# Parts of 576, 768 and 768 tokens in the feed-forward stage, in place of three of 704

## The reference

```
z = rms_norm(x, g) @ w_in;  u, q, k, v = column groups of z
h = x + concat(pool_mixer(u), banded_attention(q, k, v)) @ w_out
hn = rms_norm(h, norm_ffn)
y = h + (silu(hn @ w_gate) * (hn @ w_up)) @ w_down
```

## Time and profile before

| | us |
|---|---|
| median of 3 runs | 2101.21 |
| profiled execution | 2103.07 |
| its span, first to last instruction | 2101.3 |
| TensorE matmul busy | 2075.9 (99%) |
| VectorE busy | 1277.1 (61%) |
| ScalarE busy | 884.0 (42%) |
| GpSimd busy | 777.9 (37%) |

### The profile page before, as it was taken

How to read it: one execution, slowest core, us unless ns; L and a number is a source line. 1 busy time by engine, 2 the same in 40 slices (tenths; PEclk the granted TensorE clock), 3 DMA queues, 4 the chain that set the end, 5 groups by cost and what they waited for, 6 DMA issues and landing times.

```text
span 2101.3 us, 33467 instructions
## 1 busy us (share of the span) xinstructions
PE 2075.9 (99%) x12470; PEld 1885.5 (90%) x12470; DVE 1277.1 (61%) x2070; ACT 884.0 (42%) x2149; POOL 777.9 (37%) x503
## 2 busy tenths in 40 slices
PE   8999999999999999999999999999999999999999
PEld 7888888877888899999998999999998999999997
DVE  5655555553222566766666766766667767666665
ACT  6766666653334533333333433333334333333331
POOL 0000000034324544354435653445445643544352
PEclk9999999999999999999999999999999999999999
DMA  7011111033774532333224523333224422222222
GB/s 189 29 41 41 39 39 41 24 101 112 219 243 148 171 108 89 110 106 109 78 77 151 189 88 108 108 106 90 95 81 159 161 81 70 72 81 72 70 80 75
DMA packets 243401, 212.89 MB, mean 101 GB/s; under 512 B 21149, under 2 KB 220618, under 8 KB 243242
## 3 DMA queue, kind: packets, MB, share of 16 engines
q1 hardware_dynamic: 243242, 210.76, 32.6%
HBM read 170.03 MB, written 40.79 MB: 100 GB/s over the span
## 4 chain that ended last, share of the span: by engine, by line
PE 93%; ACT 2%; DVE 1%; issue 1%; SPq 1%; DMA 1%; POOL 0%; DVEq 0%; ACTq 0%; POOLq 0%
PE ps L813 27%; PE ps L815 27%; PE ps L814 27%; PE ps L914 2%; PE ps L888 2%; PE ps L1030 1%; PE ps L900 1%; PE ps L832 1%; SPq L466 1%; PE ps L1032 1%; PE ps L1028 1%; PE ps L876 1%; ACT s_sb L1208 1%; PE ps L931 1%; PE ps L940 0%
## 5 line engine op out<-in xcount | busy, mean ns | idle before, releaser
L746 POOL TENSOR_TENSOR w_lo<-w_lo_raw,w_hi 128x512 fp32r<-128x512 f32 (+1 forms) x240 | 393.3, 1645 | 606.5 <-PE ps L815 412.7
L813 PE MATMUL ps<-xs_hi,w_hi 128*128 128x352 f32 x1848 | 596.5, 323 | 3.6 <-POOL w_lo L746 2.8
L815 PE MATMUL ps<-xs_lo,w_hi 128*128 128x352 f32 x1848 | 597.8, 324 | 0.0
L813 PEld LDWEIGHTS ps<-xs_hi,w_hi 128*128 128x128 f32 x1848 | 347.6, 188 | 5.7 <-POOL w_lo L746 3.1
L815 PEld LDWEIGHTS ps<-xs_lo,w_hi 128*128 128x128 f32 x1848 | 351.0, 190 | 0.0
L1718 DVE TENSOR_TENSOR h<-ps,h 128x512 f32<-128x512 f32 (+1 forms) x396 | 270.3, 688 | 118.4 <-PE ps L815 112.1
L814 PE MATMUL ps<-xs_hi,ws_lo 128*128 128x352 f32 x1056 | 339.6, 322 | 0.0
L746 POOL TENSOR_TENSOR ws_lo<-ws_lo_raw,w_hi 128x512 fp32r<-128x512 f32 x204 | 295.3, 1449 | 112.2 <-DVE ws_lo_raw L1561 68.4
L1275 ACT ACTIVATE w_hi<-ws_lo_raw 128x512 fp32r<-128x512 f32 x264 | 165.5, 628 | 326.2 <-DVE ws_lo_raw L1561 326.0
L813 PE MATMUL ps<-w_hi,act_hi 128*128 128x512 f32 x660 | 257.2, 390 | 2.6 <-DVE act_lo L1641 2.6
L814 PE MATMUL ps<-w_hi,act_lo 128*128 128x512 f32 x660 | 256.9, 389 | 0.0
(11 more groups left out here) (142 smaller groups left out, 3248.0 us busy)
## 6 DMA issues: line engine op xcount, KB each, us to landing
w_lo_raw<-in_w_gate SPq DMA_DIRECT2D x66, 512.0 KB, 5.1
w_lo_raw<-in_w_up SPq DMA_DIRECT2D x66, 512.0 KB, 5.2
w_lo_raw<-in_w_down SPq DMA_DIRECT2D x66, 512.0 KB, 4.1
xload<-in_x_prompt SPq DMA_DIRECT2D x16, 512.0 KB, 4.2
mix_d<-o_st SPq DMA_DIRECT2D x64, 128.0 KB, 1.8
xt_lo_raw<-mix_d SPq DMA_DIRECT2D x16, 512.0 KB, 6.0
wg_hi_raw<-in_x_prompt SPq DMA_DIRECT2D x16, 512.0 KB, 5.1
h_d<-wg_hi_raw SPq DMA_DIRECT2D x16, 512.0 KB, 2.6
```

The costliest lines, as they stand in the source:

```text
L746: nc.gpsimd.tensor_tensor(lo, raw, hi.bitcast(F32), ALU.subtract).then_inc(done, 1)
L813: nc.tensor.matmul(out, s_hi, m_hi, start=first, stop=False, skip_group_check=partial)
L815: return nc.tensor.matmul(out, s_hi, m_lo, start=False, stop=final, skip_group_check=partial)
```

## The change

The parts now have 576, 768 and 768 tokens (`T_OF`), and products 288, 384 and 384 columns (`NB_OF`). 576 is 4 x 128 + 64, and 768 is 6 x 128: only part 0 has a tile of 64 rows. The last tile of the last part holds 64 prompt tokens and the 64 sample tokens and is stored by two transfers. Tiles in SBUF are sized for the largest part; the high and low token blocks share one array of 14 slots, and the low block of product 6 of part 0 lies in unused columns of the high slots 3 to 6. For that the high blocks 3 to 6 of part 1 wait for the last product of part 0 (`rows_high`). The weight buffers lie elsewhere, so `load_down(0)` is issued behind the last `store_hn` and the wait for `h_stored`, and three waits on the output projection's last products (`wo_free`) are moved by a step. At the joint behind part 0, `accumulate` makes low block 4 before the additions of the tile of 64 rows.

```diff
@@ -53,13 +53,17 @@
-PARTS = 3
-T = TOKENS // PARTS
-NB = T // 2
+T_OF = (576, 768, 768)
+FIRST = (0, 576, 1344)
+PARTS = len(T_OF)
+NB_OF = tuple(n // 2 for n in T_OF)
+T, NB = max(T_OF), max(NB_OF)
+HALF_TILE = T_OF[0] // PART
-PT_TILES = 6
-D_UNITS = 2 * PT_TILES
+TILES_OF = tuple(-(-n // PART) for n in T_OF)
+PT_TILES = max(TILES_OF)
@@ -253,13 +257,12 @@
+                sb("between", [PART, 1312], scope=project)
-            xs_hi = sb("xs_hi", [PART, PRODUCTS, HALF_K, NB], F32R, scope=ffn)
-            xs_raw, xs_lo = twin("xs_lo", [PART, PRODUCTS, HALF_K, NB], ffn)
-            sb("rest", [PART, PART], scope=ffn)
+            xs_raw, xs_split = twin("xs", [PART, 2 * PRODUCTS, HALF_K * NB], ffn)
@@ -268,15 +271,15 @@
-            act_hi = sb("act_hi", [PART, 2, T + DEC], F32R, scope=ffn)
+            act_hi = sb("act_hi", [PART, 2, T], F32R, scope=ffn)
+            odd = twin("w2_lo1", [PART, 2, 2, HALF_K * PART], ffn)
+            sb("gap", [PART, PART], scope=ffn)
+            even = twin("w2_lo0", [PART, 2, 2, HALF_K * PART], ffn)
-            odd = twin("w2_lo1", [PART, 2, 2, HALF_K * PART], ffn)
-            sb("gap", [PART, 960], scope=ffn)
-            even = twin("w2_lo0", [PART, 2, 2, HALF_K * PART], ffn)
@@ -407,11 +410,18 @@
-            return (DEC if j == PT_TILES - 1 else PART), T * p + PART * j
+            return min(PART, T_OF[p] - PART * j), FIRST[p] + PART * j
-            return y_sample[0] if a == SEQ else y_prompt[0, a:a + rows, :]
+            end = min(a + rows, SEQ)
+            both = [(y_prompt[0, a:end, :], 0, end - a)]
+            return both + ([(y_sample[0], end - a, rows)] if a + rows > SEQ else [])
+        def y_stores(p, j):
+            return sum(len(y_rows(b, j)) * (1 + ((b, j) == (PARTS - 1, LAST_TILE))) for b in range(p) if j < TILES_OF[b])
...
@@ -449,14 +462,33 @@
-            return xs_raw[:, m]
+            return lows_of(xs_raw, p, m)
+        def block_in(t, p, slot):
+            return t[:, slot, 0:HALF_K * NB_OF[p]].rearrange("p (k n) -> p k n", k=HALF_K)
+        def xs_hi(p, m):
+            return block_in(xs_split, p, m)
+        def lows_of(t, p, m):
+            if p == 0 and m == PRODUCTS - 1:
+                return t[:, 3:3 + HALF_K, HALF_K * NB_OF[0]:(HALF_K + 1) * NB_OF[0]]
+            return block_in(t, p, PRODUCTS + m)
+        def xs_lo(p, m):
+            return lows_of(xs_split, p, m)
-            return (0, 1, 2, 3, 5, 4) if G == NG - 1 else tuple(range(PT_TILES))
+            return (0, 1, 2, 3, 5, 4) if G == NG - 1 else tuple(range(TILES_OF[G // GROUPS]))
+        def d_units(G):
+            return sum(2 * TILES_OF[g // GROUPS] for g in range(G))
-            return D_UNITS * G + 2 * tiles_of(G).index(j) + nh
+            return d_units(G) + 2 * tiles_of(G).index(j) + nh
...
@@ -662,7 +695,7 @@
-                need(sp, d_ready, D_UNITS * G)
+                need(sp, d_ready, d_units(G))
@@ -711,10 +744,10 @@
                     load_gate_up(0)
                 if i == 7:
                     load_first_rows()
-            load_down(0)
             store_hn(NTILES - 1)
             for b in range(3):
                 sp.wait_ge(h_stored[b], 16 * len(range(b, NTILES, 3)))
+            load_down(0)
             for b in range(2):
                 sp.wait_ge(hn_stored[b], 16 * len(range(b, NTILES, 2)))
             for G in range(NG):
@@ -732,11 +765,11 @@
+                    for i in range(TILES_OF[p]):
...
@@ -961,7 +994,7 @@
-                    if i == NTILES - 1 and nh == 1 and c in (1, 4):
+                    if i == NTILES - 1 and nh == 1 and c in (1, 3, 4):
...
@@ -1011,14 +1044,14 @@
-                    pe.wait_ge(al_done, 4 * G + (3 if PART * (j + 1) <= NB else 4))
+                    pe.wait_ge(al_done, 4 * G + (3 if PART * (j + 1) <= NB_OF[G // GROUPS] else 4))
-                        if j < PT_TILES - 1:
+                        if (G // GROUPS, j) != (0, HALF_TILE):
@@ -1265,7 +1298,7 @@
-                    act.wait_ge(wo_free, 1)
+                    act.wait_ge(wo_free, 1 if m < 4 else 2)
@@ -1275,14 +1308,15 @@
-                    act.wait_ge(product_done, after_product(last_set(p), m))
+                    act.wait_ge(product_done, after_product(last_set(p), PRODUCTS - 1 if p == 1 and m >= 3 else m))
...
@@ -1317,7 +1351,8 @@
-                nc.scalar.activation(act_hi[:, c, NB * l:NB * (l + 1)], aa[:, n % 2, :], ACT.Copy).then_inc(ah_done, 1)
+                nb = NB_OF[G // GROUPS]
+                nc.scalar.activation(act_hi[:, c, nb * l:nb * (l + 1)], aa[:, n % 2, 0:nb], ACT.Copy).then_inc(ah_done, 1)
@@ -1550,7 +1585,7 @@
-                    dve.wait_ge(wo_free, 1 if n == 0 else 2)
+                    dve.wait_ge(wo_free, 2 if n == 0 else 3)
...
@@ -1587,58 +1622,62 @@
-                if l == 1:
-                    nc.vector.tensor_tensor(hi[:, T:T + DEC], aa[:, n % 2, NB - DEC:NB], hi[:, T - DEC:T].bitcast(F32),
+                if l == 1 and G < GROUPS:
+                    nc.vector.tensor_tensor(hi[:, t:t + DEC], aa[:, n % 2, nb - DEC:nb], hi[:, t - DEC:t].bitcast(F32),
...
@@ -1705,9 +1744,11 @@
+                        if j == HALF_TILE and TILES_OF[p] == HALF_TILE + 1:
+                            rows_low(p + 1, j)
-                        dve.wait_ge(h_loaded[j], 16 * (p + 1))
+                        dve.wait_ge(h_loaded[j], 16 * sum(j < TILES_OF[b] for b in range(p + 1)))
```

More of the change, by code:

```diff
@@ L430, in last_set, with part_of @@
             return 2 * GROUPS * p - 1
+        def part_of(s):
+            return s // (2 * GROUPS)
         def product_bank(s, m):
-            return ps[:, 4 + (3 * s + BANK_OF[m]) % 4, 0:NB]
+            return ps[:, 4 + (3 * s + BANK_OF[m]) % 4, 0:NB_OF[part_of(s)]]
         def low_of(s, m):
@@ L570, in rows_block @@
             def rows_block(p, j, l):
-                a = T * p + NB * l
-                return hn_k[:, HALF_K * j:HALF_K * (j + 1), a:a + NB]
+                a = FIRST[p] + NB_OF[p] * l
+                return hn_k[:, HALF_K * j:HALF_K * (j + 1), a:a + NB_OF[p]]
             def rows_stored(p):
-                last = (T * (p + 1) - 1) // PART
+                last = (FIRST[p] + T_OF[p] - 1) // PART
                 for b in range(2):
@@ L584, in load_first_rows @@
                 for m, j, l in ((0, 0, 0), (4, 0, 1), (3, 1, 0), (6, 1, 1)):
-                    load(xs_raw[:, m], rows_block(0, j, l), xs_loaded)
+                    load(rows_raw(0, m), rows_block(0, j, l), xs_loaded)
             def next_rows(p, j):
@@ L625, in load_blocks @@
                     sp.wait_ge(product_done, after_product(last_set(p), m))
-                    load(xs_raw[:, m], src, block_loaded[m])
+                    load(rows_raw(p, m), src, block_loaded[m])
             def store_y(p):
@@ L630, in store_y @@
                 for j in tiles_of(G):
-                    rows = part_rows(p, j)[0]
                     if (p, j) == (PARTS - 1, LAST_TILE):
@@ L635, in store_y @@
                             sp.wait_ge(d_free, d_index(G, j, nh) + 1)
-                            sp.dma_start(y_rows(p, j)[:, cols], h[0:rows, j, cols]).then_inc(y_stored[j], 16)
+                            for to, a, b in y_rows(p, j):
+                                sp.dma_start(to[:, cols], h[a:b, j, cols]).then_inc(y_stored[j], 16)
                     else:
                         sp.wait_ge(d_free, d_index(G, j) + 2)
-                        sp.dma_start(y_rows(p, j), h[0:rows, j]).then_inc(y_stored[j], 16)
+                        for to, a, b in y_rows(p, j):
+                            sp.dma_start(to, h[a:b, j]).then_inc(y_stored[j], 16)
             def load_h(p, j):
                 rows, a = part_rows(p, j)
-                need(sp, y_stored[j], 16 * p)
+                need(sp, y_stored[j], 16 * y_stores(p, j))
                 for b in range(3):
@@ L734, in _ @@
                     load_gate_up(2 * G + 2)
-                    for i in range(PT_TILES):
+                    for i in range(TILES_OF[p]):
                         load_h(p, i)
@@ L760, in first_rows_low @@
                 pool.wait_ge(x_sum, 1 if m == 1 else 4)
-                low(xs_high, X_HIGHS.index(m) + 1, xs_lo[:, m], xs_raw[:, m], xs_hi[:, m], xs_split_pool)
+                low(xs_high, X_HIGHS.index(m) + 1, xs_lo(0, m), rows_raw(0, m), xs_hi(0, m), xs_split_pool)
             def mix_low(i):
@@ L989, in product @@
                     cols = slice(PART * k, PART * (k + 1))
-                    last = split_products(product_bank(s, m), w2_hi[:, m, cols], lo[:, cols], xs_hi[:, m, k], xs_lo[:, m, k],
+                    last = split_products(product_bank(s, m), w2_hi[:, m, cols], lo[:, cols], xs_hi(p, m)[:, k], xs_lo(p, m)[:, k],
                                           m < 3 and k == 0, k == HALF_K - 1, partial=True)
@@ L1295, in rows_high @@
                     act.wait_ge(xs_loaded, 16 * 4)
-                nc.scalar.activation(xs_hi[:, m], rows_raw(p, m), ACT.Copy).then_inc(xs_high, 1)
```

(15 more changed lines are left out.)

27 lines of the change are left out of this document (15 added, 12 removed).

## The result

| | median of all runs, us | ratio to the kernel before, 95% interval |
|---|---|---|
| before | 2101.2 (12 runs, 2098.6 to 2104.17) | |
| after | 2108.8 (12 runs, 2106.37 to 2113.35) | 1.0037 [1.003, 1.0044] |

The kernel became 7.6 us slower, where 4.2 us less were forecast; the time lies above the predicted range. The profiled execution has a span of 2106.8 us, 5.5 more than before, at a mean granted clock of 0.997, as before.

The account below looks back on a forecast made before the run. TensorE, busy nearly the whole span, was taken as the bound. -10.0 (columns) + 1.0 + 3.2 + 2.3 (steps 2 to 4) - 0.7 (second joint) = -4.2 us, from 2101.21 to 2097.0 us, range 2091.5 to 2102.5.

Parts of the forecast that it names:

- The columns: Down projection: 2200 matmuls of 512 columns instead of 2244, all saved on TensorE's path, -10.0 us.
- Step 2: Part 0's steady groups: product 3 waits for the copy of product 0; 0.1 us for 9 groups, +1.0 (0 to 2.7).
- The margin is just zero: Part 0's even sets: the copy ends at E + 4.66, so TensorE starts product 3 at E + 4.79, as needed.
- E: Start of an even set of part 0, from which the forecast counts its times in us.
- the row: VectorE's instruction sequence in part 0, worked out from the first sum to the copy's end at E + 4.66.
- rival 2: Part 0: VectorE asks for the last activation product after GpSimd's third instruction begins; +11 us, up to 2108; chance 0.10.
- Step 3: Stage start: longer wait for gate weights, TensorE resuming at 716.4 (2.3 us), plus 0.9 at set 2's product 3; +3.2.
- Rival 3: Start: about 3.2 us idle brings half clock, costing 1.5 us and swallowing the 0.9 at product 3; 2097.7 us; chance 0.15.
- Step 4: Joint of parts 0 and 1: 1.2 us more wait at the down projection, 1.1 at the second sum; +2.3 (0.5 to 3.5).
- The second joint: Joint of parts 1 and 2: with longer sets its wait shrinks by 0.7 us.

Follow-up runs that it names:

- e7: Kernel before, leaving out 44 down-projection matmuls of 512 columns in the third part (measurement only): 2092.81 us, ratio 0.9958.
- e5: Kernel after with parts of 704, 768 and 640 tokens instead of 576, 768, 768: 2094.89 us, ratio 0.9968.
- e3: Kernel after without the second 64-column VectorE subtraction per group in part 0 from group 1 on (measurement only): 2105.64 us, one run.
- e1: Kernel after with the gate weights of set 2 issued ahead of the down weights of group 0: 2108.82 us, ratio 1.0028.
- e2: Kernel after with VectorE forming product 2's sum ahead of token block 5's low part at the joints: 2108.85 us, ratio 1.003.
- e4: Kernel after, GpSimd writing zeros instead of its four low parts in part 0's even sets but the first (measurement only): 2104.19 us, one run.
- e6: Kernel after with product 2's sum in set 1 made ahead of the first weight sum of set 2: 2108.32 us, ratio 1.0037.
- e8: Kernel after with the edits of e6, e2 and e4 together (measurement only): 2100.89 us, ratio 0.9997.
- e10: Kernel after with parts of 704, 640 and 768 tokens, the short part in the middle: 2098.12 us, ratio 0.9982.
- e9: Kernel after with the edits of e1, e2 and e4 together (measurement only): 2096.63 us, ratio 0.9976.
- e11: e5 with the gate weights of set 2 issued ahead of the down weights of group 0: 2093.44 us, ratio 0.9958.

## Why the prediction was wrong

- **The columns, -10.0: right.** Count, spacing and place on the path hold (e7, e5).
- **Step 2, the steady part, +1.0: this step failed, +6.0 measured.** "The margin is just zero" held in set 2, where the copy ended at E + 4.62 (worked out: 4.66). In the nine steady groups it ended at E + 4.86 and product 3 was 0.2 late: the row had VectorE waiting for GpSimd, but not GpSimd waiting for VectorE at its first instruction (1.53 us for 1.29). I took 0.1 a group where the bound said 0.3, and ended the row at the copy. Behind it the last low part lost its turn to GpSimd's fourth instruction in six groups, and the sums for products 5 and 4 stand behind that: the other 0.5 us. The upper bound of 2.7 us therefore left this wait out altogether. The prediction names two instructions of VectorE that wait for GpSimd in the trace of before, not the third, the short subtraction, which took 0.67 us there (896.80); it spends a whole turn (e3). The mechanism is that of rival 2, at half its price and at another place: rival 2 had the last product of activations come after the start of GpSimd's third instruction, and it still came before (E + 2.49 against E + 3.20). How many groups lose the turn (six here, four to eight in the other profiles) no row of before could tell. The trace agrees with the Trainium skill, SBUF — State Buffer, section Who interferes with whom: VectorE's subtractions with two SBUF inputs wait until a GpSimd instruction ends (0.73, 0.96, 1.57 us), its sums that read PSUM don't (0.45).
- **Step 3, the start, +3.2: 4.8 measured.** The forecast of the wait's end was good (resumed at 716.4 by the forecast, 716.14 measured), in part by luck: the weights landed 1.4 and not 1.2 us earlier, but the whole stage started 0.7 earlier, which the forecast had as before. So the wait grew by 2.8 and not 2.3. Missing was the half clock behind it, 1.5 us. Rival 3 named it at that price and held that it would swallow the 0.9 at product 3 of set 2. That wait was indeed 0.04 us, but 0.6 came at product 4 by the turns of step 2. The e1 run shows why one wait hid another here.
- **Step 4, the first joint, +2.3: 4.7 measured.** The idle part was 4.4 against about 3.8 expected: 2.2 at the projection (forecast 2.7) and 2.15 at the second sum (forecast 1.1). Two low parts in a row, put together so that the short tile's additions wait, took 4.52 us where I had counted 2 x 1.74, again GpSimd's turns. Another 1.6 are half clock, which I had weighed at the start alone.
- **The second joint, -0.7.** Its wait is 0.5 shorter, right in sign; small gaps behind it take that back.

Two of the three misses, steps 2 and 4, have one cause: the cost of GpSimd's turns was put in where the trace of before showed them and not where the shorter set would move them, and in step 2 the row was followed only to the point where TensorE first waits. Beside it stands the half clock, 3.1 us in two places.

## What to carry to other kernels

When work is divided so that some repeated stage gets shorter, list first the work of that stage which doesn't shrink, and follow the busiest helper's order through to the last instruction that TensorE waits for, not only the first. Where two engines wait for each other, write down both rows. Take the saving where the stage has room: the same 44 matmuls came with +7.6 us where the short part has 288 columns and stands in front, and with -6.9 where it has 320 and stands at the end. Before an edit is judged by the total, look whether the place it mends covers another wait or lies beside one that varies.

## What the runs showed of the hardware

- A wait of TensorE can be paid again in clock: 1.5 us behind one of 3.75, 1.6 behind one of 2.15. After gaps of 3.5 to 5.0 us in set 1 (the kernel after, e2, e3, e4, e6, e8) the granted clock was 0.50 for some 3 to 6 us; after 1.00 and 1.67 us (e1, e5) it stayed at 1.00.
- In between, the length of the gap alone doesn't decide. At the first joint 2.15 us brought the half clock in the kernel after (0.56 in the stretch shown) and in e4, and 2.15 us in e6 didn't, nor did 2.09 in e1 and 3.11 in e3. In e10 it came after 2.02 us in set 1. Behind the 2.8 to 3.1 us of idle time at the stage's own start all runs have it but e2 and e10. What does decide is open. By the Trainium skill, TensorE: Matmul & The Clock Gate, section Why this matters for your kernels, gaps between bursts can send the clock back; the rows agree for all gaps of 3.5 us and more.
- VectorE instructions that want two SBUF operands wait for GpSimd one by one: 0.73 us for 64 columns and then 1.57 for the 288 behind it. GpSimd's subtractions wait for VectorE as well (1.53 and 1.61 us for 1.29). When both begin within 0.03 us the printed starts don't tell who goes first: GpSimd at 1049.08 went ahead of 1049.11, but at 1013.68 it was behind 1013.70. Beside a write of GpSimd VectorE's took 0.46 us (e4), as alone.
- The second load of the gate weights took 7.07 us from issue to landing when 1 MB of down weights was issued ahead (kernel after, 707.04 to 714.11), and 6.7 to 8.2 in the seven other runs with that order (e2 to e6, e8, e10), against 5.40 before, 5.20 in e7, and 5.5 to 5.6 with the gate weights first (e1, e9, e11). In the chain of e5:

```profile
709.11 6.74 DMA w_lo_raw<-in_w_gate
```
